# The input stream laid out by features for the first norm, its copy by tokens behind the third weight tile

## The reference, cut to what matters

```python
def rmsnorm(x, g):
    xf = x.astype(jnp.float32)
    y = xf * lax.rsqrt(jnp.mean(xf * xf, axis=-1, keepdims=True) + NORM_EPS)
    return (y * g.astype(jnp.float32)).astype(x.dtype)
...
        h = rmsnorm(x, norm1_g[i])
        mix = hybrid_mixer(h, w_in[i], ...)
        x = x + mix @ w_out[i]
```

## Time and profile before

| | |
|---|---|
| median of 3 runs | 1029.92 us (1029.65 to 1030.87) |
| the profiled execution | 1029.68 us |
| span of its trace | 1028.4 us |
| instructions in the trace | 14767 |
| HBM read | 177.16 MB |

### The profile page before, as it was taken

One profiled execution on the slowest core, in us unless ns is written; L12 is line 12 of the kernel. 1 busy time (PEld: TensorE's weight loads), 2 busy tenths in 40 slices (PEclk: granted clock), 3 DMA queues, 4 the chain that ended last, 5 costly groups with the idle time before them and its releaser, 6 DMA issues.

```text
span 1028.4 us, 14767 instructions
## 1 busy us (share of the span) xinstructions
PE 1016.7 (99%) x5712; PEld 853.9 (83%) x5714; DVE 759.2 (74%) x1210; ACT 553.2 (54%) x837; POOL 224.0 (22%) x311
## 2 busy tenths in 40 slices
PE   8999999999999999999999999999999999999997
PEld 6877788888888877788888888997888878888886
DVE  6987678788777887668787778988745457666665
ACT  6575656555456475666554556746534554434432
POOL 0270600000000271600000003118967620000000
PEclk9999999999999999999999999999999999999999
DMA  9451455555554361355655544453445555555541
GB/s 358 152 201 50 142 185 176 198 181 202 195 198 160 127 216 42 124 211 184 226 184 184 205 166 163 168 200 103 160 153 198 206 184 226 181 207 185 181 148 41
DMA packets 26822, 179.16 MB, mean 174 GB/s; under 512 B 2944, under 2 KB 3072, under 8 KB 6272
## 3 DMA queue, kind: packets, MB, share of 16 engines
q1 hardware_dynamic: 26752, 178.22, 49.3%
HBM read 177.16 MB, written 1.05 MB: 173 GB/s over the span
## 4 chain that ended last, share of the span: by engine, by line
PE 95%; POOL 2%; issue 1%; DMA 1%; DVE 1%; ACT 0%; SPq 0%; DVEq 0%; POOLq 0%
PE pb L697 17%; PE pb L702 10%; PE pb L577 9%; PE pb L578 8%; PE pb L580 8%; PE pb L720 6%; PE pb L722 6%; PE pb L721 6%; PE pb L703 2%; PE pb L958 2%; PE pb L914 2%; POOL wlo L2616 2%; PE pb L926 1%; PE pb L659 1%; PE pb L624 1%; PE pb L622 1%
## 5 line engine op out<-in xcount | busy, mean ns | idle before, releaser
L1780 DVE TENSOR_TENSOR wlo<-raw,whi 128x2048 fp32r<-128x2048 f32 x127 | 290.6, 2290 | 108.3 <-ACT whi L1304 108.0
L1304 ACT ACTIVATE whi<-raw 128x2048 fp32r<-128x2048 f32 (+1 forms) x164 | 304.9, 1863 | 61.9 <-PE pb L580 31.5
L2616 POOL TENSOR_TENSOR wlo<-raw,whi 128x256 fp32r<-128x256 f32 x260 | 196.9, 795 | 320.4 <-ACT whi L1304 320.4
L697 PE MATMUL pb<-hb,whi 128*128 128x512 f32 x770 | 194.0, 391 | 0.0
L697 PEld LDWEIGHTS pb<-hb,whi 128*128 128x128 f32 x770 | 145.0, 188 | 28.7
L577 PE MATMUL pb<-whi,hb 128*128 128x512 f32 x344 | 137.5, 400 | 1.2 <-issue 0.8
L578 PE MATMUL pb<-wlo,hb 128*128 128x512 f32 x344 | 134.1, 390 | 0.0
L580 PE MATMUL pb<-whi,hb 128*128 128x512 f32 x328 | 128.1, 391 | 0.0
L702 PEld LDWEIGHTS pb<-hb,wlo 128*128 128x128 f32 x880 | 120.1, 190 | 8.6
L702 PE MATMUL pb<-hb,wlo 128*128 128x256 f32 x880 | 122.7, 282 | 0.0
L720 PE MATMUL pb<-whi,gh 128*128 128x512 f32 x280 | 109.4, 391 | 0.0
(11 more groups left out here) (390 smaller groups left out, 1545.3 us busy)
## 6 DMA issues: line engine op xcount, KB each, us to landing
raw<-wst SPq DMA_DIRECT2D x160, 1024.0 KB, 4.8
raw<-wst SPq DMA_DIRECT2D x8, 512.0 KB, 3.9
gb<-gains SPq DMA_DIRECT2D x3, 512.0 KB, 5.7
X<-x SPq DMA_DIRECT2D x2, 512.0 KB, 5.7
out<-X SPq DMA_DIRECT2D x4, 256.0 KB, 2.1
PQ<-prm SPq DMA_DIRECT2D x1, 909.0 KB, 4.5
raw<-wst SPq DMA_DIRECT2D x2, 256.0 KB, 7.5
prmt<-prm SPq DMA_DIRECT2D x1, 479.0 KB, 10.3
```

The costliest lines, as they stand in the source:

```text
L697: e.matmul(both, wh[:, k, s], hb2[:, k, :, :].rearrange("p i q -> p (i q)"), start=k == 0, stop=False)
L1304: e.activation(whi[:, split_slot(m), 0:w], raw[:, m % RAW, 0:w], ACT.Copy).then_inc(*hi(m))
L1780: e.tensor_tensor(wlo[:, split_slot(m), 0:w], raw[:, m % RAW, 0:w], whi[:, split_slot(m), 0:w].bitcast(F32), ALU.subtract).then_inc(*lo_v(m))
L2616: g = e.tensor_tensor(wlo[:, split_slot(m), s], raw[:, m % RAW, s], whi[:, split_slot(m), s].bitcast(F32), ALU.subtract)
```

## The change

Another input, `xt`, holds x by features: 128 rows, feature 128 k + p in row p, 8 x 256 columns. It is loaded in two halves of 512 KB into the buffer XN (seen there as `scaled`), and ScalarE and VectorE make the high and low parts of the stream from it (`high_laid`, `low_laid`). The sixteen turnings of the first norm go. x by tokens is still needed, for the squares and for the sums later; it is loaded whole behind tile 2, and all four squares are ScalarE's. The loads come in this order now: 56 columns of parameters (the gain and the tables of the rotation), half of xt, tile 0 in halves, half of xt, tile 1 in halves, tile 2, x, tile 3, the identity, the other parameters, and the masks as before. Tile 0 is split in quarters and tiles 1 and 2 in halves; for tile 0 TensorE goes in pairs of k over both groups of tokens, all high parts first (`very_first`). Five warm-up matmuls stand together. On VectorE and ScalarE tile 2 is split ahead of the squares' end, tile 3 behind the eviction (on VectorE behind the indexer's rope). The 16-column rope goes from VectorE to POOL in both layers, and TensorE waits for it there (`roped_g`).

```diff
-FIRST = 136
+FIRST = (128, 184)
...
-    at, n = {"ident": (0, 128), "n10": (128, 8)}, FIRST
+    at, n = {"ident": (0, 128), "n10": (128, 8)}, FIRST[0] + 8
+    for name, w in (("cosh", 16), ("sinh", 16), ("cosi", 8), ("sini", 8)):
+        at[name] = (n, w)
+        n += w
+    assert n == FIRST[1]
...
-            return x_new[("down", l - 1), t, h] if l else (s_xh[h], 16)
+            return x_new[("down", l - 1), t, h] if l else (s_x, 16)
...
+            def very_first(m, banks, ready):
+
+                wh, wl = (w.rearrange("p (k c) -> p k c", k=4) for w in parts(m))
+                for pair in range(2):
+                    for t in range(2):
+                        s, o = slice(128 * t, 128 * t + 128), PB[banks[t]][:, :]
+                        bank_free(banks[t])
+                        for k in (2 * pair, 2 * pair + 1):
+                            q.wait_ge(*(hi[m] if k == 3 else hi["quarter", k]))
+                            q.wait_ge(*ready[k])
+                            e.matmul(o, hh[:, k, s], wh[:, k, :], start=k == 0, stop=False)
+                            e.matmul(o, hl[:, k, s], wh[:, k, :], start=False, stop=False)
+                for t in range(2):
+                    s, o = slice(128 * t, 128 * t + 128), PB[banks[t]][:, :]
+                    for k in range(4):
+                        q.wait_ge(*(lo_v[m] if k == 3 else lo_v["quarter", k]))
+                        mm = e.matmul(o, hh[:, k, s], wl[:, k, :], start=False, stop=False)
+                    mm.then_inc(*(used(m) if t else half_used(m)))
...
-                    keep_warm(2, 3)
-                    turn_half(("n1", 0), 0, 0, 1)
-                    keep_warm(1, 6)
+                    keep_warm(5, 3)
...
                 def transposed(first, last):
+                    q.wait_ge(s_ident, 16)
...
-                    weights_high_first(first, 0, 0, True, (hi["first"], hi[first]), n1,
-                                       lambda: turn_half(("n1", l), 1, 0, 1))
-                    tokens_half(first, 1, 1, 0, True, False, n1)
+                    very_first(first, (0, 1), n1)
                     second = tile_at[l, "in", 0, 1]
-                    weights_high_first(second, 0, 4, False, (hi[second], hi[second]), n1)
+                    weights_high_first(second, 0, 4, (hi["half", second], hi[second]), n1)
...
-                q.wait_ge(*roped[l, "kb"])
+                q.wait_ge(*roped_g[l, "kb"])
...
+                def high_laid(h):
+                    q.wait_ge(s_first, 16)
+                    q.wait_ge(s_xt[h], 16)
+                    for b in (2 * h, 2 * h + 1):
+                        for k in (2 * b, 2 * b + 1):
+                            a = e.activation(hh[:, k, :], scaled[:, k, :], ACT.Copy, scale=par("n10")[:, k:k + 1])
+                        a.then_inc(*hh_done(("n1", 0), b))
+
+                def split_halves(m):
+                    for c in range(0, CH, 1024):
+                        q.wait_ge(*(landed(m) if c or m > 1 else (s_half[m], 16)))
+                        e.activation(whi[:, m, c:c + 1024], raw[:, m, c:c + 1024],
+                                     ACT.Copy).then_inc(*(hi(m) if c else hi("half", m)))
+
                 if l == 0:
-                    high_half(("n1", 0), 0, par("n10"))
-                    for c in range(0, CH, 1024):
-                        q.wait_ge(*(landed(0) if c else (s_half, 16)))
-                        e.activation(whi[:, 0, c:c + 1024], raw[:, 0, c:c + 1024],
-                                     ACT.Copy).then_inc(*(hi(0) if c else hi("first")))
-                    high_half(("n1", 0), 1, par("n10"))
-                    split(1)
+                    high_laid(0)
+                    for k in range(4):
+                        s = slice(512 * k, 512 * k + 512)
+                        q.wait_ge(*(landed(0) if k >= 2 else (s_half[0], 16)))
+                        e.activation(whi[:, 0, s], raw[:, 0, s], ACT.Copy).then_inc(*(hi(0) if k == 3 else hi("quarter", k)))
+                    high_laid(1)
+                    split_halves(1)
+                    split_halves(2)
+                    q.wait_ge(*hl_done[("n1", 0), 7])
+                    square_half(("n1", 0), 0)
                     square_half(("n1", 0), 1)
+                    project(0, 0, 0)
+                    ahead(l, "in", 0, 1)
...
+                def low_laid(h):
+                    for b in (2 * h, 2 * h + 1):
+                        q.wait_ge(*hh_done[n1, b])
+                        for k in (2 * b, 2 * b + 1):
+                            e.scalar_tensor_tensor(hl[:, k, :], scaled[:, k, :], par("n10")[:, k:k + 1],
+                                                   hh[:, k, :].bitcast(F32), ALU.mult, ALU.subtract).then_inc(*hl_done(n1, k))
+
+                def split_halves(m):
+                    for c in range(0, CH, 1024):
+                        s = slice(c, c + 1024)
+                        q.wait_ge(*(hi[m] if c else hi["half", m]))
+                        v = e.tensor_tensor(wlo[:, m, s], raw[:, m, s], whi[:, m, s].bitcast(F32), ALU.subtract)
+                    v.then_inc(*lo_v(m))
...
-                    q.wait_ge(s_xh[0], 16)
-                    for t in range(2):
-                        xs = X[:, t, 0:512]
-                        v = e.scalar_tensor_tensor(XN[:, t, 0:512], xs, 1.0 / D, xs, ALU.mult, ALU.mult,
-                                                   accum_out=norm_of[n1][:, 2 * t:2 * t + 1])
-                    v.then_inc(*dve("squares"))
-                    q.wait_ge(s_first, 16)
-                    low_half(n1, 0, par("n10"))
-                    for c in range(0, CH, 1024):
-                        q.wait_ge(*(hi[0] if c else hi["first"]))
-                        s = slice(c, c + 1024)
-                        v = e.tensor_tensor(wlo[:, 0, s], raw[:, 0, s], whi[:, 0, s].bitcast(F32), ALU.subtract)
-                    v.then_inc(*lo_v(0))
-                    low_half(n1, 1, par("n10"))
-                    split(1)
-                    q.wait_ge(*dve["squares"])
-                    for t in range(2):
-                        q.wait_ge(*squares[n1, t, 1])
-                        mean(n1, t)
+                    low_laid(0)
+                    for k in range(4):
+                        s = slice(512 * k, 512 * k + 512)
+                        q.wait_ge(*(hi[0] if k == 3 else hi["quarter", k]))
+                        e.tensor_tensor(wlo[:, 0, s], raw[:, 0, s], whi[:, 0, s].bitcast(F32),
+                                        ALU.subtract).then_inc(*(lo_v(0) if k == 3 else lo_v("quarter", k)))
+                    low_laid(1)
+                    split_halves(1)
+                    split_halves(2)
+                    means(n1)
...
+                q.wait_ge(s_first, 16)
+                rope(e, q, rt, dve, roped(l, "ik"), C_IQ, 9, 32, 4, "cosi", "sini")
+                if l == 0:
+                    ahead(l, "in", 0, 1)
                 q.wait_ge(s_prm, 16)
-                rope(e, q, rt, dve, roped(l, "ik"), C_IQ, 9, 32, 4, "cosi", "sini")
-                q.wait_ge(*roped[l, "ik"])
-                rope(e, q, rt, dve, roped(l, "kb"), C_KB, 1, 64, 8, "cosh", "sinh")
...
                 root(("n1", l))
+                for t in range(2):
+                    q.wait_ge(*proj(l, 0, t))
+                q.wait_ge(s_first, 16)
+                rope(e, q, rt_g, pool, roped_g(l, "kb"), C_KB, 1, 64, 8, "cosh", "sinh")
                 m = ahead_to(m, l, "in", 2, 1)
                 for t in range(2):
                     q.wait_ge(*proj(l, 2, t))
-                q.wait_ge(s_prm, 16)
+                q.wait_ge(*roped_g[l, "kb"])
...
+            def load_xt(h):
+                e.dma_start(XN[:, h, :], xt[:, 1024 * h:1024 * h + 1024]).then_inc(s_xt[h], 16)
+
+            def load_halves(m):
+                e.dma_start(raw[:, m, 0:CH // 2], wst[m, :, 0:CH // 2]).then_inc(s_half[m], 16)
+                e.dma_start(raw[:, m, CH // 2:CH], wst[m, :, CH // 2:CH]).then_inc(s_raw[m], 16)
...
-            e.dma_start(prmt[:, 0:FIRST], prm[:, 0:FIRST]).then_inc(s_first, 16)
-            load_x(0)
-            e.dma_start(raw[:, 0, 0:CH // 2], wst[0, :, 0:CH // 2]).then_inc(s_half, 16)
-            e.dma_start(raw[:, 0, CH // 2:CH], wst[0, :, CH // 2:CH]).then_inc(s_raw[0], 16)
-            load_x(1)
-            load(1)
-            e.dma_start(prmt[:, FIRST:], prm[:, FIRST:]).then_inc(s_prm, 16)
+            e.dma_start(prmt[:, FIRST[0]:FIRST[1]], prm[:, FIRST[0]:FIRST[1]]).then_inc(s_first, 16)
+            load_xt(0)
+            load_halves(0)
+            load_xt(1)
+            load_halves(1)
+            load(2)
+            e.dma_start(X[:, :, :], x[0].rearrange("(t p) c -> p t c", t=2)).then_inc(s_x, 16)
+            load(3)
+            e.dma_start(prmt[:, 0:FIRST[0]], prm[:, 0:FIRST[0]]).then_inc(s_ident, 16)
+            e.dma_start(prmt[:, FIRST[1]:], prm[:, FIRST[1]:]).then_inc(s_prm, 16)
             second = tile_at[1, "up", 2, 0]
```

(5 more changed lines are left out.)

38 lines of the change are left out of this document (16 added, 22 removed).

## The result

The change made the kernel slower: 1034.01 us median (1029.76 to 1039.27, 20 runs) against 1030.2 us for the kernel before in the same batch (1029.65 to 1033.73, 20 runs), a ratio of 1.003 with a 95% interval of [1.0016, 1.0043]. The forecast was 1028.9 us in a range of 1027.8 to 1030.1.

The account below looks back on a forecast made before the run. TensorE, busy 99% of the span, was taken as the bound: it starts 1.86 us earlier, VectorE's lateness cuts that to 1.0 us, giving 1028.7, plus 0.24 for the median: 1028.9 us, range 1027.8 to 1030.1.

Parts of the forecast that it names:

- Step (d): First layer's GELU on VectorE: ends 0.41 us early, at 59.36 us, so TensorE starts L973 at 59.45, 1.0 us ahead.
- rival B: POOL's small rope is caught behind VectorE's split of tile 3; L773 starts at 26.0 us, gain 0.7 us, 1029.2 us; chance 0.19.
- s: VectorE's lateness from its split of tile 4 on, because that tile lands later: 0.65 us.
- rival D: Added megabyte loads at the slow early rate, tile 4 lands at 27.6 us, kernel slower at 1031.9 us; chance 0.08.
- 1.66 - s: What VectorE's idle time lets through at the GELU; the gain is the smaller of this and TensorE's 1.86 us.
- (c): POOL's low part of tile 9, eight of 16 pieces, ends at 56.2 us, just as TensorE wants it: cost 0.
- TensorE's 1.86 us: How much earlier TensorE reaches the turnings of L773, ready at 24.8 us: 0.43 + 1.50 - 0.07.
- The turnings' 1.50 us: Eight turnings of X between the first projection's matmuls, with the waits around them, all go: 1.50 us saved on TensorE.
- The start's 0.43 us: First projection starts at 8.30 us instead of 8.73, as ScalarE's first piece has 512 columns instead of 1024.
- (b): Second indexer: a ReLU released by VectorE ends at 39.55 us, TensorE asks at 39.1, waits, and is 1.2 us ahead.
- C: Clock stays low in the warm-up block, ten passes last to 10.3 us, nothing gained, 1029.9 us; chance 0.07.

Follow-up runs that it names:

- tail and rope: Changed kernel with the GELU's last VectorE instructions using PSUM operands and VectorE's split of tile 3 waiting for POOL's small rope: 1029.9 us median.
- the first experiment: Changed kernel with one operand moved: the GELU's last product on VectorE takes its second input from PSUM instead of SBUF: 1034.07 us.
- the longer row: Kernel before with two more POOL pieces, into a scratch tile, between the two tiles of the row: 1031.37 us; with the GELU tail in PSUM 1031.26 us.

## Why the prediction was wrong, point by point

- **Step (d) failed.** It put the GELU at three short VectorE instructions with the durations of the earlier trace rows and shifted it as a block. I had laid VectorE's and POOL's orders side by side for the small rope (rival B) but not for the GELU, though the earlier trace rows show a POOL piece running across 59 us. The same port that B names cost TensorE nothing in the profiled execution of before (L2011 took 0.49 us there, 0.16 with its input in PSUM), and held the product for 3.46 us in this one. No rival had it, and so the forecast gave slower only 0.06. None of the three runs shown of before was over 1030.87 us, so nothing but the rows pointed at it.
- **The price of being shut out was not in the rows.** The earlier trace rows show one POOL piece caught behind one VectorE split, and the prediction works with that alone: wait for the one instruction that is running. By it a caught GELU would have cost 0.7 us at most. The other way round VectorE waited for all the pieces left in the row, five of them (3.46 us against 0.70 us from piece to piece).
- **s was mis-sized**, 1.49 us instead of 0.65: tile 4 landed 0.8 us later than forecast (25.4 us). X came 0.8 us late too (18.4 us against 17.65). The early loads ran slower than the 2.49 us a megabyte that I took for the added 1024 KB. This is rival D's mechanism at less than half its size. With the GELU freed, this lateness and rival B together took the gain and no more (1030.33 us). By the forecast's own rule, 1.66 - s, 0.17 us would have been left for VectorE to give. But this lateness also moved POOL's row from 49.98 to 51.45 us, and so raised the price of a caught GELU from about 3 us (the late runs of before) to 4 us and over, as more pieces are left behind the product (3.4 us of the row against 2.2). POOL stood in (c) with only its first eight pieces; the other eight were in no step.
- **TensorE's 1.86 us were 1.1 to 1.3.** The turnings' 1.50 us went, as forecast: 72 matmuls from 8.87 to 25.40 us in the trace with tail and rope are 16.53 us against 16.52 forecast. The start's 0.43 us did not come. The first weights were in at 8.2 us instead of 7.6, at the bad end of the half microsecond either way that I had priced at 0. One slip in the sum does not matter: 20.1 us and 1.08 us for the two powers are 21.2 us, not 21.05.
- **Rival B came true**, to the letter in its mechanism: five small rope instructions at 0.22 to 0.32 us (I took 1.2 us for the six), the sixth caught behind the split, 2.30 us. As X was late, it was over at 26.35 us, L791 stood at 26.61 us instead of B's 26.0, and the start was worth 0.07 us instead of B's 0.7. Here the rule of the Trainium skill that the prediction cites, a shared read port held by whichever starts first, agreed with the trace. It should have raised B's chance above 0.19: both ropes wait for the same evictions, six instructions each, and the split stands right behind VectorE's.
- **The rule for carrying a gain held.** The forecast said 1.0 us at L973, at 59.45 us, limited by VectorE and not by TensorE. With both faults cured L989 stands at 59.55 us, 0.91 us ahead, and with one of them cured at 60.21 and 60.39 us. The wait at the second indexer, (b), appeared in the run with the late tile, 0.54 us.
- **C**, the clock in the warm-up, did not decide in any trace here: the ten passes ended at 7.75 us after the change, and at 8.4 to 8.7 us in the four traces of the changed kernel with its GELU tail in PSUM, each time ahead of the first weights. It was close in the first experiment, where they ended at 8.47 us and the first projection began at 8.54 us.
- The medians: with the GELU out of the way the changed kernel took 1030.33 us. So of the 5.1 us between forecast and result, 1.4 us are the start and tile 4, and 3.7 us the caught GELU.

## What to carry to other kernels

When a change makes one engine's block of work later, lay the new order over its neighbour's on the shared port and look for every short VectorE instruction on the critical path that reads only SBUF and falls under a row of back-to-back POOL instructions; price it not at one POOL instruction but at up to what is left of the row, and with a chance, since it happens in some runs and not in others. Where it can be had, a PSUM operand takes such a chain off the port at no cost (0.16 to 0.24 us for each of the three here), and here this was surer than moving the row, which met the next instruction of the kind. And look at all runs before the median: groups a few microseconds apart mean an event that happens or not, and a profile shows only one of the outcomes.

## What the runs showed of the hardware that was not expected

- A VectorE instruction that reads only SBUF can be shut out for a whole row of POOL instructions, not for one: 3.46, 3.42, 3.77, 3.96 and 3.71 us for a product on 32 columns and 3.05 us for a scaling of 16 columns, each ending within 0.1 us of the row's end, while a piece came every 0.70 us as before. In other traces the same instructions waited for one piece at most (0.68 and 0.49 us). At the scaling of the exponentials one VectorE instruction got in per piece: the four took 2.56 us, 0.64 us each, 1.7 us into the next row, and 2.57 us where POOL waited for the GELU, 2.4 us into a row. What makes the difference is not known. The Trainium skill (SBUF — State Buffer, "Who interferes with whom") says that whichever starts first holds the pair "for the whole instruction"; that explains one piece, and these runs add that the one that waits need not be next.
- The other way, POOL's 16-column instruction took 2.30 us behind one split of 2.29 us.
- TensorE's granted clock fell to 0.50 (1.2 GHz) after it stood for 2.59 us in the changed kernel, and came back about 3.4 us later; after 2.46 us in the kernel before with the longer row it fell too, and came back only after some 13.6 us; after 2.9 and 3.0 us in the kernels with two and three added instructions it came back after some 10 and 13.6 us; after 2.16 us in the first experiment it stayed at 1.00. So the caught runs of the changed kernel and its variants cost about 4 us or 7 to 9 us, for stands of 2.2 to 3.0 us in the profiled ones.
- Early loads: xt's first half was in about 1 us later than x's first half before (ScalarE begins on it at 5.99 us; VectorE began at 4.94 us), though issued among the first and in longer packets. What slows them was not looked into.
